# Indexer scores of the last two token tiles over two sets of PSUM banks, and the first convolution slab behind them

## The chip, the cores and the metric

The kernel runs on one core of a Trainium2 chip. The metric is the device time of one launch, in microseconds (us), lower is better; it is given as the median of three runs. The engines are named as the profile names them: PE is TensorE (PEld its weight loads), ACT is ScalarE, DVE is VectorE, POOL is GpSimd, SP the engine that issues the weight loads from memory.

## What is computed

Two layers of a hybrid encoder over 1,072 tokens (1,024 of a prompt, 16 meta tokens, 32 new frames of a running stream). Each layer starts like this:

```python
z = rms_norm(x) @ w_in          # -> q, k, v, indexer qi (4 heads), ki, wi, conv B, C, x, gates A, B
s = einsum('bqhd,bld->bqhl', qi, ki) * IDX_DIM ** -0.5
score = einsum('bqh,bqhl->bql', wi, relu(s))        # sum over the 4 indexer heads
idx = top_k(where(admissible, score, -inf), topk)   # 256 keys (40 for the running stream)
o = attention over the chosen keys                  # branch A
y_b = (cb * causal_conv3(cc * cx)) @ w_conv_out     # branch B
```

The branches are gated, merged and projected, and an MLP (1,024 to 4,096 and back) follows.

## The kernel before

**Layout.** Every engine has its program written out by hand, with semaphores between them; each engine works its own instructions off strictly in the order of the code. Matmuls take fp32r operands, each weight and activation is split into a high and a low part, and three products are added (high by high, high by low, low by high).

**Projection and scores.** The loop `for n in range(9)` in the PE program goes over nine token tiles in the order of `ORDER`: n = 0 is the special tile (meta tokens and stream), then the eight prompt tiles. In turn n, PE runs the projection of tile n + 2 (`proj`, L621, PSUM banks 0 to 2) in four quarters, and between them `turn` (L635: transposes into banks 3 and 4) and `scores` (L651) for the four indexer heads h of tile n. The scores of one head fill up to 1,040 columns from column 2560, that is banks 5 to 7. At n = 7 and n = 8 no projection is left. ACT reads the scores out of PSUM with a relu (`relu_scores`, L1061) into one of two buffers, R0 or R1; DVE multiplies by the head's weight and adds into SC (`add_scores`, L1612 and L1615). PE counts on the semaphore `idx_relu`: the scores of a head wait until the relu of the head before it is done, since both use banks 5 to 7. ACT's program in turn n also copies the projection out of banks 0 to 2 (`copy_out(n + 1)`, semaphore `sb_copied`), copies the transposes, issues stores, and stages the next tile. The copy out of the last tile is the first thing that ACT does in turn n = 7.

**Slabs.** After the scores PE runs 12 convolution slabs and 16 gate slabs (L519, 72 matmuls of 358 columns each, 8 steps of k with 9 matmuls each). Slabs take turns between banks 0 to 2 and 3 to 5. In the kernel before, the first four k steps of slab 0 stand ahead of the scores of tile 8, head 3, and the last four behind them. Slab i waits for its weights (`slab_in`: POOL splits a slab into high and low, L407 and L409, and may start the one for slab 1 only when all 32 adds of the scores are done, `idx_added`), and for its banks: slab 3 waits for DVE's product of `conv_input(0)`, slab 4 for DVE's `conv_gate(0)` (both L1646, semaphore `conv_drained`).

**The search on DVE.** When the last add is done, DVE starts to search the top-k threshold of every row by 31 bits, one pass (L1764, six counts) a bit. The convolution's elementwise work stands at fixed places in that search: `conv_input(j)` and `conv_gate(j)` behind the passes 3j + 2 and 3j + 3 (passes over SC counted from the first bit), `conv_lo_part` between them. The masks that the search gives are read when attention begins, behind the last gate slab. `mask_row` (L1827) is DVE's first step of attention, `logits` (L763) PE's.

Of the kernel before, what the change touches and what calls it, by code (L numbers as in the profile page):

```python
# [21 lines left out]
ALU, ACT, AX = mybir.AluOpType, mybir.ActivationFunctionType, mybir.AxisListType  # L22
# [9 lines left out]
KT = D_MODEL // P  # L32
# [18 lines left out]
S_CONV, S_GATE = 0, NCONV  # L51
# [9 lines left out]
EXT = [N_META + P * (i + 1) for i in range(SPECIAL)] + [MS + PAST]  # L61
# [17 lines left out]
def pieces(t):  # L79

    if t == SPECIAL:
        return [(0, META0, EXT[t])]
    out, c = [(0, META0, N_META)], N_META
    while c < EXT[t]:
        n = min(512 - c % 512, EXT[t] - c)
        out.append((c, c - N_META, n))
        c += n
    return out


def key_tiles(t):

    if t == SPECIAL:
        return [(0, META0, MS, SPECIAL), (MS, PAST0, PAST, SPECIAL + 1)]
    return [(N_META + P * j, P * j, P, j) for j in range(t + 1)] + [(0, META0, N_META, SPECIAL)]
# [29 lines left out]
def edge_no(l, w, i):  # L125

    if l == 0:
        return i
    return 12 * l - 3 + (2 * i + (w == 0) if l < DEPTH else i)


def side(i):
# [10 lines left out]
def build(nc, d):  # L143
    ctx = ExitStack()
    with ctx:
        names = set()

        def sem(name):
            assert name not in names
            names.add(name)  # L150
            return ctx.enter_context(nc.semaphore(name))
# [142 lines left out]
        def ch(ap):  # L294
# [3 lines left out]
        flat = PS[:, :, :].rearrange("p b n -> p (b n)")  # L298
# [9 lines left out]
        slab_done = sem("slab_done")  # L308
# [9 lines left out]
        proj_done, sb_copied, roped, st_hi, st_lo = (  # L318
            sem("proj_done"), sem("sb_copied"), sem("roped"), sem("st_hi"), sem("st_lo"))
# [5 lines left out]
        idx_done, idx_relu, idx_added = sem("idx_done"), sem("idx_relu"), sem("idx_added")  # L325
# [181 lines left out]
        def _(pe):  # L507
            def slab(l, i, s, b0, act, ks=range(KT), signal=True):

                ks = list(ks)  # L510
                for k in ks:
                    last = slab_step(s, b0, act, k, k == ks[0], k == ks[-1])
                last.then_inc(slab_done if signal else half_done, 1)

            def slab_step(s, b0, act, k, first, last):

                for w, a in ((0, 0), (0, 1), (1, 0)):
                    for c in range(NCH):
                        mm = nc.tensor.matmul(PS[:, b0 + c, 0:CW], W[:, s, w, k, :],  # L519
                                              act[:, a, k, c * CW:(c + 1) * CW],  # L520
                                              start=(first and w == 0 and a == 0), stop=(last and w == 1))
                return mm

            def item(w, bank_, j, c, act, ks, first, last):

                for k in ks:
                    for h, a in ((0, 0), (0, 1), (1, 0)):
                        mm = nc.tensor.matmul(PS[:, bank_, 0:CW], w[:, h, k, :], act[:, a, k, c * CW:(c + 1) * CW],  # L528
                                              start=(k == first and h == 0 and a == 0), stop=(k == last and h == 1))
                return mm  # L530
# [35 lines left out]
            def slab_in(l, i):  # L566
                pe.wait_ge(raw_split, l * NRAW + KT + i + 3)
# [33 lines left out]
            for l in range(DEPTH):  # L601
# [26 lines left out]
                def turn(n, blocks, b0, evacs):  # L628

                    m = ROWS[ORDER[n]]  # L630
                    if evacs:
                        pe.wait_ge(turned_out, l * 36 + evacs)
                    for i, blk in enumerate(blocks):
                        o = (b0 + i // 4) * 512 + (i % 4) * P
                        last = nc.tensor.matmul(flat[:, o:o + m], ST[0:m, blk, :], identr[0:m, 0:m],  # L635
                                                start=True, stop=True)
                    last.then_inc(turned, 1)

                def scores(n, h):
                    t = ORDER[n]  # L640
                    m = ROWS[t]
                    if t not in RANKED:
                        return
                    j = RANKED.index(t)
                    if h == 0:
                        pe.wait_ge(turned_out, l * 36 + 4 * n + 2)
                    if 4 * j + h:
                        pe.wait_ge(idx_relu, l * 32 + 4 * j + h)
                    for dst, key, w in pieces(t):
                        for x in range(2):  # L650
                            last = nc.tensor.matmul(flat[0:m, 2560 + dst:2560 + dst + w],  # L651
                                                    IQ[:, h, 0:m], IK[:, x, key:key + w],
                                                    start=(x == 0), stop=(x == 1))
                    last.then_inc(idx_done, 1)
# [23 lines left out]
                for n in range(9):  # L678

                    pe.wait_ge(st_hi, (l * 9 + n + 1) * 3)  # L680
                    pe.wait_ge(st_lo, (l * 9 + n + 1) * 3)
                    turn(n, [8, 9, 10, 11, 12, 13], 3, 4 * n)
                    proj(n + 2, range(0, 2))
                    turn(n, range(8), 3, 4 * n + 2)
                    scores(n, 0)
                    proj(n + 2, range(2, 4))
                    turn(n, range(14, 18), 3, 4 * n + 3)
                    scores(n, 1)
                    proj(n + 2, range(4, 6))
                    scores(n, 2)  # L690
                    proj(n + 2, range(6, 8))
                    if n == 8:
                        slab_in(l, S_CONV)
                        pe.wait_ge(sb_copied, (l + 1) * 9)
                        for k in range(4):
                            slab_step(0, 0, H, k, k == 0, False)
                    scores(n, 3)


                for j in range(4):  # L700
                    for w in range(3):
                        i = 3 * j + w
                        if i == 0:
                            for k in range(4, KT):
                                last = slab_step(0, 0, H, k, False, k == KT - 1)
                            last.then_inc(slab_done, 1)
                            continue
                        slab_in(l, S_CONV + i)

                        if i == 1:  # L710
                            pe.wait_ge(turned_out, (l + 1) * 36)
                            pe.wait_ge(idx_relu, (l + 1) * 32)
                        else:
                            jj, ww = divmod(i - 2, 3)
                            if ww == 0:
                                pe.wait_ge(cc_drained, l * 4 + jj + 1)
                            else:
                                pe.wait_ge(conv_drained, l * 8 + 2 * jj + ww)
                        slab(l, i, i % 2, 3 * (i % 2), H)
# [7 lines left out]
                for s in range(2):  # L727
                    slab_in(l, S_GATE + NGATE - 2 + s)
                    pe.wait_ge(gates_drained, (l + 1) * NGATE - 1 + s)
                    for k in range(KT):  # L730
                        last = slab_step(s, 3 * s, H, k, k == 0, k == KT - 1)
# [70 lines left out]
                for u, (a, kv, kt) in enumerate(STEPS):  # L802
                    i, n = NKV * a + kv, len(key_tiles(ORDER[a]))
# [23 lines left out]
                for k in range(KT):  # L827
                    pe.wait_ge(m_hi, l * NMERGE + k + 1)
                    pe.wait_ge(m_lo, l * NMERGE + k + 1)
                    for c in range(NCH):  # L830
                        last = item(W[:, 0], c, 0, c, H, [k], 0, KT - 1)
                        if k == KT - 1:
                            last.then_inc(item_done, 1)
                for n, (j, c) in enumerate(ITEMS):
# [5 lines left out]
                    last = item(WR[:, j - 1], n % 6, j, c, H, range(KT), 0, KT - 1)  # L840
# [68 lines left out]
                for s in range(2):  # L909
                    slab_in(l, S_MLP + 2 + s)  # L910
                    pe.wait_ge(up_drained, l * NFB * 8 + 2 + s + 1)
                    for k in range(KT):
                        if s == 0 and k == 4:
                            chunk_broadcast(l, 5)
                        last = slab_step(s, 3 * s, H, k, k == 0, k == KT - 1)
# [12 lines left out]
                for k in range(KT):  # L928
                    pe.wait_ge(a_hi, (l * NFB + NFB - 1) * 8 + k + 1)
                    pe.wait_ge(a_lo, (l * NFB + NFB - 1) * 8 + k + 3)  # L930
                    for i in range(NCH):
                        last = item(W[:, 0], i, 0, SIDES[i], A, [k], 0, KT - 1)
# [32 lines left out]
        def _(act):  # L965
# [82 lines left out]
            for l in range(DEPTH):  # L1048
# [3 lines left out]
                def relu_scores(n, h):  # L1052
                    m, t = ROWS[ORDER[n]], ORDER[n]
                    if t not in RANKED:
                        return
                    j = RANKED.index(t)
                    act.wait_ge(idx_done, l * 32 + 4 * j + h + 1)
                    if 4 * j + h >= 2:
                        act.wait_ge(idx_added, l * 32 + 4 * j + h - 1)
                    dst = (R0, R1)[h % 2]  # L1060
                    nc.scalar.activation(dst[0:m, 0:EXT[t]], flat[0:m, 2560:2560 + EXT[t]], ACT.Relu)\  # L1061
                        .then_inc(idx_relu, 1)

                def copy_out(n):
# [55 lines left out]
                for n, t in enumerate(ORDER):  # L1120
                    m, nn = ROWS[t], l * 9 + n
# [28 lines left out]
                    for h in range(1, NIDX):  # L1150
                        relu_scores(n, h)
# [66 lines left out]
                for u, (a, kv, kt) in enumerate(STEPS):  # L1218
                    t, now = ORDER[a], NKV * a + kv
                    m, w, n = ROWS[t], key_tiles(t)[kt][2], len(key_tiles(t))  # L1220
# [39 lines left out]
                for s in range(2):  # L1260
                    n = l * NMERGE + NMERGE - 2 + s
# [835 lines left out]
```

## Time and profile before

| what | value |
|---|---|
| median of three runs | 3534.87 us (3533.64 to 3535.16) |
| profiled execution, own time | 3524.78 us |
| profiled execution, span | 3523.0 us |
| mean granted TensorE clock | 0.968 of full |
| PE busy | 3345.7 us, 95% of the span |
| DVE, POOL, ACT busy | 1876.1, 1123.8, 769.5 us |
| scores (L651) | 336 matmuls, two layers |
| relu of scores (L1061) | 64 activations, median 0.655 us |

A line of the timeline gives the start and the length of a group of instructions, the engine, the source line, the operation and its shapes, and in brackets how long the engine had stood idle before it and who ended the idle time. The granted clock is told as a share: 1.00 is 2.4 GHz, 0.50 is 1.2 GHz. The scores of the last two tiles of the first layer lie at about 217 to 250 us of the span, those of the second layer at about 1953 to 1988 us.

### The profile page before, as it was taken

Reading aid. Unit: us, or ns where it says so; the run is one execution under the profiler, and the core shown is the slowest. Engines: PE = TensorE matmul, PEld = TensorE weight load, DVE = VectorE, ACT = ScalarE, POOL = GpSimd, SP = SyncE. Lnnn points to the kernel's source line nnn. Section 1 sums busy time; section 2 is a strip of 40 time slices with the busy share of each in tenths; the row PEclk is TensorE's granted clock in tenths of the full one; section 3 lists DMA queues with packets and bytes.
Section 4 is the critical chain, followed back from the end, with each engine's and each line's share of the span. In section 5 each row is a group of like instructions: output and inputs, shape, how many; then the busy total and the mean of one; then the engine's idle time right before and its main releaser. Section 6 shows DMA issues by size and latency. Waiting matters only on the chain.

```text
span 3523.0 us, 49297 instructions
## 1 busy us (share of the span) xinstructions
PE 3345.7 (95%) x19604; PEld 3177.9 (90%) x19604; DVE 1876.1 (53%) x3093; ACT 769.5 (22%) x1368; POOL 1123.8 (32%) x517
## 2 busy tenths in 40 slices
PE   4989998999999999999969899989999999999997
PEld 3989998669999999999969899976699999999997
DVE  5249997654563242415562599966446623333255
ACT  4330111560330010101233201125413201001011
POOL 2013333004544343434420233320045434344360
PEclk8989998999999999999989899979999999999998
DMA  3111223003321111111331112220133211111113
GB/s 124 49 55 42 67 86 122 25 7 136 110 75 42 45 45 42 48 42 48 103 98 56 53 42 80 85 103 25 41 110 99 79 48 42 48 42 48 42 60 101
DMA packets 95743, 230.00 MB, mean 65 GB/s; under 512 B 11921, under 2 KB 52465, under 8 KB 95601
## 3 DMA queue, kind: packets, MB, share of 16 engines
q1 hardware_dynamic: 33552, 122.57, 11.1%
q10 hardware_dynamic: 62048, 105.48, 8.6%
q8 instruction: 97, 1.59, 0.2%
q14 instruction: 46, 0.37, 0.0%
HBM read 176.37 MB, written 51.65 MB: 65 GB/s over the span
## 4 chain that ended last, share of the span: by engine, by line
PE 86%; DVE 7%; ACT 2%; issue 2%; DMA 2%; POOL 1%; ACTq 1%; DVEq 0%; POOLq 0%
PE PS L519 58%; PE PS L528 9%; PE PS L621 6%; PE PS L792 5%; PE PS L763 3%; PE PS L780 2%; PE PS L651 2%; DVE PASS L1764 1%; PE PS L635 1%; DVE X L1538 1%; DVE HN L1493 1%; DMA HN<-x_keep 1%; DVE X L1544 1%; ACT SB L967 1%; DVE H L1489 1%
## 5 line engine op out<-in xcount | busy, mean ns | idle before, releaser
L519 PE MATMUL PS<-H,W 128*128 128x358 f32 x8352 | 1385.9, 328 | 11.3 <-DVE CB L1646 7.3
L519 PEld LDWEIGHTS PS<-H,W 128*128 128x128 f32 x8352 | 1381.3, 190 | 13.2 <-issue 10.3
L407 POOL TENSOR_TENSOR W<-RAW,ones 128x1024 fp32r<-128x1024 f32 x188 | 365.7, 1945 | 2051.7 <-PE PS L519 1664.6
L519 PE MATMUL PS<-A,W 128*128 128x358 f32 x4608 | 760.9, 327 | 0.0
L519 PEld LDWEIGHTS PS<-A,W 128*128 128x128 f32 x4608 | 759.5, 189 | 1.5 <-issue 1.5
L409 POOL TENSOR_TENSOR W<-RAW,W 128x1024 fp32r<-128x1024 f32 x188 | 522.0, 2777 | 14.8
L1764 DVE TENSOR_SCALAR_CACHE_REDUCE PASS<-SC,TC,CST 128x400 bf16<-128x400 f32 x372 | 356.0, 1019 | 1.7
L621 PE MATMUL PS<-WQ,H 128*128 128x364 f32 (+1 forms) x1296 | 244.3, 345 | 45.7 <-ACT SB L967 38.5
L621 PEld LDWEIGHTS PS<-WQ,H 128*128 128x128 f32 (+1 forms) x1296 | 218.4, 190 | 57.8 <-ACT SB L967 41.4
L1927 DVE TENSOR_TENSOR SQ<-SQ,RS 128x1074 f32<-128x1074 f32 x64 | 117.8, 1840 | 266.0 <-ACT SQ L1338 260.2
L1338 ACT ACTIVATE SQ<-PS 128x1074 f32<-128x1074 f32 x64 | 68.4, 1068 | 811.2 <-PE PS L519 808.9
L1929 DVE TENSOR_TENSOR SQ<-SQ 128x1074 f32<-128x1074 f32 x64 | 205.1, 3204 | 2.2
L1942 DVE TENSOR_TENSOR X<-X,PS 128x1074 f32 x32 | 40.8, 1274 | 307.3 <-PE PS L519 307.3
L792 PE MATMUL PS<-PT,V 128*128 128x512 f32 (+3 forms) x368 | 197.9, 621 | 0.3
L763 PEld LDWEIGHTS PS<-KS,QS 128*128 128x128 f32 (+1 forms) x704 | 116.9, 208 | 82.5 <-issue 65.8
L763 PE MATMUL PS<-KS,QS 128*128 128x16 f32 (+6 forms) x704 | 169.8, 371 | 13.0 <-issue 8.0
L528 PE MATMUL PS<-A,WD 128*128 128x358 f32 x1008 | 168.1, 327 | 0.0
L528 PE MATMUL PS<-H,WR 128*128 128x358 f32 x1008 | 168.0, 326 | 0.0
L528 PEld LDWEIGHTS PS<-A,WD 128*128 128x128 f32 x1008 | 165.1, 188 | 0.0
L528 PEld LDWEIGHTS PS<-H,WR 128*128 128x128 f32 x1008 | 164.5, 188 | 0.0
L967 ACT ACTIVATE PT<-PS 128x512 f32<-128x512 f32 (+3 forms) x184 | 107.4, 583 | 187.9 <-PE PS L780 187.8
L967 ACT ACTIVATE A<-SQ 128x1074 f32 (+1 forms) x64 | 70.6, 1103 | 340.9 <-DVE SQ L1929 340.9
(176 smaller groups left out, 2859.3 us busy)
## 6 DMA issues: line engine op xcount, KB each, us to landing
RAW<-in_w_slab SPq DMA_DIRECT2D x216, 512.0 KB, 3.5
gates<-GS ACTq DMA_DIRECT2D x32, 537.0 KB, 3.0
x_keep<-X ACTq DMA_DIRECT2D x9, 1432.0 KB, 7.6
RAW<-in_w_qkv SPq DMA_DIRECT2D x16, 546.0 KB, 3.6
GA<-gates ACTq DMA_DIRECT2D x16, 537.0 KB, 3.7
GB<-gates ACTq DMA_DIRECT2D x16, 537.0 KB, 4.6
ALO<-x_keep ACTq DMA_DIRECT2D x6, 1432.0 KB, 7.5
qs_keep<-QH ACTq DMA_DIRECT2D x16, 512.0 KB, 2.6
```

The source lines that it names most:

```text
L407: g_.tensor_tensor(hi, raw, one, ALU.mult).then_inc(hi_split, 1)
L409: g_.tensor_tensor(lo, raw, hi.bitcast(F32), ALU.subtract).then_inc(raw_split, 1)
L519: mm = nc.tensor.matmul(PS[:, b0 + c, 0:CW], W[:, s, w, k, :], act[:, a, k, c * CW:(c + 1) * CW], start=(first and w == 0 and a == 0), sto ...
L528: mm = nc.tensor.matmul(PS[:, bank_, 0:CW], w[:, h, k, :], act[:, a, k, c * CW:(c + 1) * CW], start=(k == first and h == 0 and a == 0), st ...
L621: last = nc.tensor.matmul(PS[0:m, b, 0:QG], H[:, a, k, t * P:t * P + m], WQ[:, k, w, b * QG:(b + 1) * QG], start=(k == 0 and w == 0 and a ...
L651: last = nc.tensor.matmul(flat[0:m, 2560 + dst:2560 + dst + w], IQ[:, h, 0:m], IK[:, x, key:key + w], start=(x == 0), stop=(x == 1))
L763: last = nc.tensor.matmul(flat[0:m, c0 + dst:c0 + dst + w], QS[:, a % 3, GROUP * kv + q, 0:m], KS[:, 2 * kv + x, key:key + w], start=(x == ...
L792: nc.tensor.matmul(PS[:, 6 + kv, 0:GROUP * m], V[0:w, vt, :], PT[0:w, u % 3, 0:GROUP * m], start=(kt == 0), stop=(kt == len(key_tiles(t)) ...
L967: return nc.scalar.activation(out, in_, ACT.Copy)
L1764: did(V_.tensor_scalar(PASS[0:m, SC_OFF[t]:SC_OFF[t] + EXT[t]], row(t), at_least, cst["negk"][0:m, c:c + 1], op, ALU.add, accum_out=CNT[0: ...
L1927: V_.tensor_tensor(SQ[:, s, :], SQ[:, s, :], RS[:, :], ALU.mult).then_inc(up_scaled, 1)
L1929: V_.tensor_tensor(SQ[:, s, :], SQ[:, s, :], SQ[:, s, :], ALU.mult).then_inc(up_sq, 1)
```

## The change

Of the tiles n = 7 and n = 8, heads 1 and 3 write their scores to banks 0 to 2 (column 0 on), heads 0 and 2 stay in banks 5 to 7. ACT's relu reads from the same column. The wait of these scores is loosened by one: from the second head of tile 7 on, a head waits for the relu before the last one. The first head that writes to banks 0 to 2 waits for the last copy out of the projection. Slab 0 is no longer cut in two: it stands whole behind the last scores and waits for all 32 relus of the layer.

```diff
+def score_col(n, h):
+
+    return 0 if n >= 7 and h % 2 else 2560
...
                     if h == 0:
                         pe.wait_ge(turned_out, l * 36 + 4 * n + 2)
+                    if n == 7 and h == 1:
+                        pe.wait_ge(sb_copied, (l + 1) * 9)
                     if 4 * j + h:
-                        pe.wait_ge(idx_relu, l * 32 + 4 * j + h)
+                        pe.wait_ge(idx_relu, l * 32 + 4 * j + h - (4 * n + h > 28))
                     for dst, key, w in pieces(t):
                         for x in range(2):
-                            last = nc.tensor.matmul(flat[0:m, 2560 + dst:2560 + dst + w],
+                            last = nc.tensor.matmul(flat[0:m, score_col(n, h) + dst:score_col(n, h) + dst + w],
...
                     proj(n + 2, range(6, 8))
-                    if n == 8:
-                        slab_in(l, S_CONV)
-                        pe.wait_ge(sb_copied, (l + 1) * 9)
-                        for k in range(4):
-                            slab_step(0, 0, H, k, k == 0, False)
                     scores(n, 3)
...
                         if i == 0:
-                            for k in range(4, KT):
-                                last = slab_step(0, 0, H, k, False, k == KT - 1)
-                            last.then_inc(slab_done, 1)
+                            slab_in(l, S_CONV)
+                            pe.wait_ge(idx_relu, (l + 1) * 32)
+                            slab(l, 0, 0, 0, H)
                             continue
...
-                    nc.scalar.activation(dst[0:m, 0:EXT[t]], flat[0:m, 2560:2560 + EXT[t]], ACT.Relu)\
+                    nc.scalar.activation(dst[0:m, 0:EXT[t]], flat[0:m, score_col(n, h):score_col(n, h) + EXT[t]], ACT.Relu)\
```

## Rows read from the trace of the kernel before

**Rows 1.** The page: its head, and the chain that ended last, by engine.
```profile
span 3523.0 us, 49297 instructions
...
PE 86%; DVE 7%; ACT 2%; issue 2%; DMA 2%; POOL 1%; ACTq 1%; DVEq 0%; POOLq 0%
```
**Rows 2.** The chain that ended last, 205 to 305 us: start, length, what.
```profile
243.19 6.91 PE PS L519 x36
...
252.47 1.31 DVE SC L1615
...
297.42 1.47 DVE CB L1646 x4
```
**Rows 3.** Waits of PE, 215 to 310 us: total, times, longest.
```profile
PE PS L651 <- ACT R L1061: 4.2, 5, 1.6
PE PS L519 <- DVE CB L1646: 3.6, 1, 3.6
...
PE PS L519 <- POOL W L409: 1.0, 1, 1.0
PE PS L519 <- DVE CU L1646: 0.9, 1, 0.9
```
**Rows 4.** Timeline of PE, tiles 7 and 8, first layer.
```profile
219.47 2.29 PE L651 MATMUL PS<-IK,IQ 128*128 128x16 f32 x6 [0.28 <-ACT R L1061]
...
223.39 2.29 PE L651 MATMUL PS<-IK,IQ 128*128 128x16 f32 x6 [1.64 <-ACT R L1061]
...
240.49 2.70 PE L651 MATMUL PS<-IK,IQ 128*128 128x16 f32 x8 [1.13 <-ACT R L1061]
243.04 7.05 PE L519 MATMUL PS<-H,W 128*128 128x358 f32 x36
249.93 1.42 PE L651 MATMUL PS<-IK,IQ 128*128 128x16 f32 x8
251.21 6.17 PE L519 MATMUL PS<-H,W 128*128 128x358 f32 x36
```
**Rows 5.** Timeline of ACT and POOL, tiles 7 and 8, first layer.
```profile
213.95 1.07 ACT L967 ACTIVATE SB<-PS 128x1092 f32<-128x1092 f32 x1
...
222.43 0.91 ACT L1061 ACTIVATE R<-PS 128x912 f32<-128x912 f32 x1
...
238.54 2.68 POOL L409 TENSOR_TENSOR W<-RAW,W 128x1024 fp32r<-128x1024 f32 x1
```
**Rows 6.** Stretches of 1 us: busy time of PE, PEld, DVE, ACT, POOL, then granted clock.
```profile
233.00:234.00 1.00, 1.00 (x5) 0.92 (x5) 0.00 (x0) 0.87 (x1) 0.00 (x0) 0.50 0.00 0
...
245.00:246.00 1.00, 1.00 (x8) 1.00 (x8) 0.60 (x1) 0.00 (x0) 0.00 (x0) 0.99 0.00 0
```
**Rows 7.** Timeline of PE, slabs 1 and 2, slab 3, slab 4 and on.
```profile
258.40 23.98 PE L519 MATMUL PS<-H,W 128*128 128x358 f32 x144 [1.02 <-POOL W L409]
283.31 12.10 PE L519 MATMUL PS<-H,W 128*128 128x358 f32 x72 [0.93 <-DVE CU L1646]
299.02 121.25 PE L519 MATMUL PS<-H,W 128*128 128x358 f32 x725 [3.61 <-DVE CB L1646]
```
**Rows 8.** Timeline of POOL and DVE at the ends of slabs 3 and 4.
```profile
295.56 1.91 POOL L407 TENSOR_TENSOR W<-RAW,ones 128x1024 fp32r<-128x1024 f32 x1 [8.36 <-PE PS L519]
295.76 1.74 DVE L1787 SCALAR_TENSOR_TENSOR TC<-TU,TC 128x8 uint32<-128x8 uint32 x1
...
304.78 0.17 DVE L1787 SCALAR_TENSOR_TENSOR TC<-TU,TC 128x8 uint32<-128x8 uint32 x1
...
312.73 1.90 POOL L407 TENSOR_TENSOR W<-RAW,ones 128x1024 fp32r<-128x1024 f32 x1 [12.81 <-PE PS L519]
```
**Rows 9.** Timeline of PE, second layer, first half of slab 0.
```profile
1979.69 7.40 PE L519 MATMUL PS<-H,W 128*128 128x358 f32 x36
```
**Rows 10.** Waits of PE, second layer, 1950 to 2052 us.
```profile
PE PS L519 <- DVE CB L1646: 3.7, 1, 3.7
```
**Rows 11.** Timeline of DVE, its first step of attention.
```profile
587.55 0.33 DVE L1827 CUSTOM_DVE_ANT_0 PA<-PS,MB 48x176 f32<-48x176 f32 x1 [5.12 <-PE PS L763]
```

## Prediction

> **What bounds the kernel now.** I read the page first: PE is on 86% of the chain that ended last, DVE on 7% [rows 1]. So time comes out of this kernel where PE idles or runs slowly, and the question is who makes it do so between the last projection and the slabs. The chain between 205 and 305 us says it: it goes through the first half of slab 0 (243.19, 6.91 us), then through the scores of tile 8, head 3, their relu and their add (252.47, 1.31 us), and then stays on DVE's search until `conv_gate(0)` (297.42, 1.47 us) [rows 2]. The reader is to see that the half slab that fills PE's wait for a relu also holds back the last add, from which DVE's whole search starts, and that slab 4 then waits for that search. The waits of PE give the sizes: 4.2 us in five waits of scores for relus, 1.0 us of slab 1 for its weights, 0.9 and 3.6 us of slabs 3 and 4 for DVE [rows 3]. The clock is the second finding: through tiles 7 and 8 PE runs at 1.2 GHz, also in a stretch in which it is busy throughout (233 to 234 us), and full clock is back at 245 us, some 2 us into slab 0 [rows 6].
>
> **What it removes, one layer.** (a) The five waits of scores for the relu of the head before: 4.2 us [rows 3]. Can the looser wait be met? Head 1 of tile 7 starts 0.28 us earlier, at 219.2 [rows 4]; its banks are free, since the last copy out began at 213.95 and took 1.07 us [rows 5]. Head 2 follows at about 221.5, by 2.29 us a head, head 3 at 223.8. Head 3 needs the relu of head 1, which ACT starts at 222.43 (it stages a tile before it, so this relu comes no earlier) and ends at 223.34 [rows 5]: just in time. In tile 8 a head takes 2.7 us on PE and the relu about 1.05 us on ACT [rows 2 and 4], so the relu before the last is always done. I take the whole 4.2.
> (b) Slab 1's wait, 1.0 us [rows 3]. Its weights can be split only after the last add. That add ends at 253.78 now [rows 2]; with scores of head 3 ahead of the slab it ends about 10 us earlier (below), and the split ends before slab 0 does.
> (c) DVE's chain. From the last add's end at 253.78 to the end of `conv_gate(0)` at 298.89 it takes 45.1 us [rows 2]. In the kernel after, slab 0 starts as the last relu ends, and the last add ends 1.3 us after that, so `conv_gate(0)` ends 46.4 us after slab 0 starts. Slab 4 is due after four slabs: slabs 1 and 2 take 23.98, slab 3 takes 12.10 [rows 7], so 48 us at full clock and about 2 us more for the start at half clock: 50. DVE is 3.6 us early, and both waits go: 0.9 + 3.6 = 4.5 us [rows 3].
> (d) What follows the wait of slab 4. Slab 3 runs from 283.31 to POOL's release at 295.56, 12.25 us; slab 4 from 299.02 to 312.73, 13.7 us [rows 7 and 8]. The only difference is that slab 4 starts after 3.61 us of idle PE. With that idle gone 1.4 us come back.
> Removed: 4.2 + 1.0 + 4.5 + 1.4 = 11.1 us.
>
> **What it adds, one layer.** (e) The scores of tile 8, head 3 now run in the half clock stretch. At half clock eight of these matmuls hold PE from 240.49 to 243.04, 2.55 us; now they hold it at full clock from 249.93 to 251.21, 1.28 us [rows 4]. Added 1.3 us.
> (f) A new wait: slab 0 waits for the relu of the scores just ahead of it. The same wait for the same size of relu stands in the row before slab 0 and lasts 1.13 us [rows 4]. Behind it on PE are all the slabs, so nothing fills it: 1.1 us. The weights of slab 0 are no wait: POOL ends their split at 241.22 now [rows 5], some 3 us earlier when the transposes before them are, against a slab start at about 242.4.
> (g) The clock at the start of the slab. Now the first half of slab 0 takes 7.05 us against 6.17 for the second half, a loss of 0.9; in the second layer 7.40, a loss of 1.2 [rows 4 and 9]. After an idle wait the loss may be like slab 4's 1.4 (d). Below, I take 0.9 again as the least; above, twice slab 4's, 2.8, since the wait comes at the end of a half clock stretch and not after full clock. I take 2.0, between, so 1.1 more than now in the first layer and 0.8 in the second.
> Added: 1.3 + 1.1 + 1.0 = 3.4 us.
> (h) Slab 0 uncut costs nothing: it has the same 72 matmuls. The wait for `sb_copied` costs nothing (a). The DMAs are as before; the weights for slab 1 can only come earlier. ACT's order is the same.
>
> **Sum.** 11.1 − 3.4 = 7.7 us a layer. As a check by places: slab 0 starts at 243.04 − 4.2 + 2.55 + 1.1 = 242.5; slab 4 at 292.5 instead of 299.02, and it ends 1.4 us sooner relative to its start, 7.9 us in all. The second layer shows the same waits, with 3.7 us for slab 4 [rows 10], and loses less at (g): 8.1 us. Together 16 us. Behind slab 4 PE runs 121 us and more without a wait [rows 7], so the gain is carried on. The masks must be ready at the start of attention: there DVE has waited 5.12 us for PE's first logits [rows 11]. DVE moves up by at least as much as PE, since it starts 10 us earlier and meets PE again at each later `conv_input`. The sum is made in the profiled execution, 3524.78 us with a span of 3523.0; the median of the runs is 3534.87, 10.1 us above it. I take the difference over unscaled: 3534.87 − 16 = 3519.
>
> **A page against the rows.** The rows show PE busy throughout and still at half clock [rows 6]; it was transposing and scoring. The Trainium skill, page "TensorE: Matmul & The Clock Gate", section "What's actually happening", says that the throttled state is the default and that activity releases it; by that rule alone closing the waits of (a) could bring full clock back among the scores, and the sum would be that of rival A. The row speaks against it for a busy PE of this mix, but no stretch of this trace has three heads in a row without a wait.
>
> **Rivals.**
> A. *Full clock comes back while PE still scores.* In the kernel after, heads 1 to 3 of tile 7 run without a gap, which no row shows. For: it is denser than anything here before slab 0. Against: the busy stretch at 0.50. Price: a head of tile 8 holds PE 1.28 instead of 2.55 us [rows 4]; with four of them, ACT's copies in between become the wait, and I count some 3 of the 5 us; the 2.0 of (g) goes as well. 5 us more a layer, 3509 with both layers, 3514 with one. It is not more, because DVE's 46.4 us then stand against 48 for PE.
> B. *DVE's chain gets longer and binds.* While POOL splits (295.56, 1.91 us) a small DVE operation took 1.74 instead of 0.17 us [rows 8]. Where such meetings fall changes with the change. Three more of them cost 3 × 1.6 = 4.8 us, 1.2 over the margin of 3.6, with 1.4 again for an idle start of slab 4; the gain is 5 to 7 us a layer, 3521 to 3525. On this, the Trainium skill, page "SBUF — State Buffer", section "SBUF: two separate sides", tells of a port pair that DVE and GpSimd lock against each other for a whole instruction; the trace agrees with 1.74 us beside 1.91.
> C. *Slower: half clock stays deep in the slabs.* The new wait (f) puts idle time right ahead of the dense work. Every us at half clock costs half a us, so the change is a loss once more than some 16 us a layer beyond the 4 us of (g) run at 1.2 GHz; slower by 7 us at 23. It would give 3542. Against: both starts of slab 0 and that of slab 4 lost at most 1.4 us.
> D. *The waits only move.* Head 3 of tile 7 meets the relu by less than half a us (a). If ACT's staging holds each relu back, 2 of the 4.2 us stay, and the gain is 6 us a layer: 3523.
>
> **How the numbers follow.** Forecast, the sum with (g) between its bounds (3516 to 3522): 0.65. A: 0.16. B and D: 0.13. C: 0.02. Nothing measurable, for a reason that I don't see, 0.04. 0.2%, about what a measurement of this kernel can tell from no change, is 7.1 us, under half of the sum; B and D still lie beyond it. So faster 0.93, same 0.05, slower 0.02. The range from 3510 to 3526 takes in (g)'s bounds, B and D and most of A.
>
> **What would show it.** The waits of L651 for R gone at tiles 7 and 8; one wait of about 1.1 us before slab 0 at about 242.5; the last add ended at about 243.8 (c); no wait of L519 for POOL, CU or CB; slab 4 at about 292.5 and of 12 us; granted clock 0.50 until 2 to 5 us into slab 0. Waits of L519 for CB would show B, full clock before slab 0 A, waits for R at tile 7 D. The forecast is wrong if DVE's chain from the last add is over 48 us, or if PE's idle time turns up again later, ahead of attention.

## The result, and the profile after

The kernel after took 3509.6 us (median of 4 runs, 3503.4 to 3510.4) beside 3534.8 us before (4 runs, 3533.6 to 3535.2): ratio 0.9926, interval 0.9908 to 0.9943. The direction was right, the size was not: 16 us were forecast, 25 came, and 3509.6 lies just outside the range, below its end of 3510. Run twice more on other occasions the kernel gave ratios of 0.9922 (0.9905 to 0.9939) and 0.9939 (0.9925 to 0.9953). Over all 16 executions its mean is 3508.8 us, over 63 of the kernel before 3533.0: 24.2 us.

The line numbers move: the scores are L658 now, the slabs L524, POOL's splits L412 and L414, the relu L1063, DVE's CU and CB L1648. The page of the kernel after, its head and the chain by engine, which answer to [rows 1]:

```profile
span 3508.1 us, 49299 instructions
...
PE 88%; DVE 5%; ACT 2%; issue 2%; DMA 1%; POOL 1%; ACTq 1%; DVEq 0%; POOLq 0%
```

DVE has lost 2 points of the chain, PE has gained them. The waits of PE in the first layer, 212 to 320 us:

```profile
PE PS L640 <- ACT IK L969: 3.8, 2, 2.0
PE PS L524 <- ACT R L1063: 2.6, 1, 2.6
PE PS L658 <- ACT R L1063: 0.8, 2, 0.4
```

and those of the second layer, 1938 to 2060 us:

```profile
PE PS L640 <- ACT IK L969: 3.0, 2, 2.0
PE PS L524 <- ACT R L1063: 1.2, 1, 1.2
PE PS L658 <- ACT R L1063: 0.3, 1, 0.3
```

Beside [rows 3] and [rows 10]: the waits for POOL, CU and CB are gone in both layers, the relu waits of the scores have shrunk from 4.2 us to 0.8 us in the first layer and 0.3 in the second, and the one new wait, slab 0 for the last relu, is 1.2 us in the second layer, as forecast, but 2.6 in the first. The timeline of PE says why. First layer, the kernel after:

```profile
219.92 3.96 PE L658 MATMUL PS<-IK,IQ 128*128 128x16 f32 x12
224.33 1.31 PE L658 MATMUL PS<-IK,IQ 128*128 128x16 f32 x6 [0.45 <-ACT R L1063]
...
230.74 2.83 PE L658 MATMUL PS<-IK,IQ 128*128 128x16 f32 x16
233.88 1.52 PE L658 MATMUL PS<-IK,IQ 128*128 128x16 f32 x8 [0.31 <-ACT R L1063]
238.04 92.25 PE L524 MATMUL PS<-H,W 128*128 128x358 f32 x542 [2.64 <-ACT R L1063]
```

Head 3 of tile 7 (224.33) takes 1.31 us where it took 2.29: from here on PE is at full clock while it still scores, which is rival A. Slab 0 starts at 238.04, 5 us before [rows 4] and 4.5 us before the forecast 242.5. The relu that it waits for was itself held, by DVE's adds. The timeline of POOL, DVE and ACT:

```profile
232.96 2.71 POOL L414 TENSOR_TENSOR W<-RAW,W 128x1024 fp32r<-128x1024 f32 x1
233.86 5.71 DVE L1617 SCALAR_TENSOR_TENSOR SC<-R,WI,SC 128x1040 f32<-128x1040 f32 x3 [0.43 <-ACT R L1063]
236.86 1.04 ACT L1063 ACTIVATE R<-PS 128x1040 f32<-128x1040 f32 x1 [2.10 <-DVE SC L1617]
```

At full clock PE outruns the adds, and R0 and R1 come free too late: ACT waits 2.10 us, PE 2.64. The first of the three adds of L1617 takes 2.90 us, the next 1.30. POOL's split of slab 0's weights (232.96 to 235.67) runs beside the slow one, so 1.6 of the 2.10 us that ACT waits are the length that this add has over the next. It is the kind of meeting that rival B names, in a place where B did not look for it. The wait costs more than its length. Stretches of 1 us of the same execution, columns as in [rows 6]:

```profile
237.00:238.00 1.00, 0.00 (x0) 0.00 (x0) 1.00 (x1) 0.90 (x1) 0.00 (x0) 0.59 0.56 176
243.00:244.00 1.00, 1.00 (x5) 1.00 (x4) 0.93 (x4) 0.00 (x0) 1.00 (x1) 0.50 0.00 0
244.00:245.00 1.00, 1.00 (x8) 1.00 (x7) 0.90 (x4) 0.00 (x0) 0.16 (x1) 0.99 0.00 0
```

While PE idles the clock falls, and slab 0 runs its first 6 us at half clock.

**How the runs are compared below.** Every run lists its span and its mean granted clock. Span × clock is the time that the execution would have taken if every stretch at half clock had been half as long; span × (1 − clock), half the time at half clock, is called below what it lost to half clock. This is bookkeeping and not yet a cause: idle time at half clock falls half into each part, though a higher clock would not shorten it. The listed clock has three digits, so one run's split is good to about 2 us, a mean's to less.

| kernel | runs | mean us | span × clock | lost to half clock (runs) |
|---|---|---|---|---|
| before | 63 | 3533.0 | 3408.0 | 123.2 (116 to 134) |
| after | 16 | 3508.8 | 3393.7 | 113.3 (101 to 123) |
| order only | 7 | 3520.0 | 3398.0 | 120.1 (112 to 127) |
| banks only | 12 | 3525.6 | 3403.7 | 120.1 (105 to 138) |
| tile 8 only | 6 | 3520.9 | 3396.5 | 122.6 (120 to 127) |
| tile 7 only | 6 | 3516.4 | 3396.9 | 117.7 (112 to 123) |
| swapped banks | 4 | 3499.3 | 3392.6 | 104.9 (98 to 112) |
| before + filler | 12 | 3529.0 | 3413.2 | 114.1 (106 to 120) |
| after + filler | 4 | 3497.0 | 3406.0 | 89.1 (87 to 95) |
| swapped + filler | 4 | 3497.3 | 3401.1 | 94.4 (87 to 98) |

So of the 24.2 us, 14.3 are in the first part and 9.9 in the second. The 9.9 are not all a gain of clock. The relu waits stood at half clock, so about half of the 8.4 us of them is in it. So are the 3 us that slab 4 ran at half clock behind its wait (granted clock 0.81, 0.50, 0.50 and 0.50 from 299 to 303 us before, 1.00 throughout slab 4 in the third profile below), 1.6 us lost in each layer. What the half clock among the scores gave or took beside these is smaller than the scatter of single executions.

### The profile page after: what moved, and what is told of

The parts are those of the page before. It is cut to its first block, busy times and chain, and to the rows that moved or that the text cites. A ratio compares the mean times of both kernels' runs of the same rounds, so it can differ in the third digit from the quotient of the medians.

```text
span 3508.1 us, 49299 instructions
## 1 busy us (share of the span) xinstructions
PE 3348.5 (95%) x19604; PEld 3181.8 (91%) x19604; DVE 1873.5 (53%) x3093; ACT 769.0 (22%) x1368; POOL 1123.9 (32%) x517
## 4 chain that ended last, share of the span: by engine, by line
PE 88%; DVE 5%; ACT 2%; issue 2%; DMA 1%; POOL 1%; ACTq 1%; DVEq 0%; POOLq 0%
PE PS L524 61%; PE PS L533 9%; PE PS L626 6%; PE PS L794 5%; PE PS L765 3%; PE PS L782 2%; PE PS L658 1%; PE PS L640 1%; DVE X L1540 1%; DVE HN L1495 1%; DVE X L1546 1%; DMA HN<-x_keep 1%; ACT SB L969 1%; DVE H L1491 1%; DVE H L1535 0%
## 5 line engine op out<-in xcount | busy, mean ns | idle before, releaser
L524 PE MATMUL PS<-H,W 128*128 128x358 f32 x8352 | 1383.3, 328 | 3.9 <-ACT R L1063 3.9
L524 PEld LDWEIGHTS PS<-H,W 128*128 128x128 f32 x8352 | 1380.8, 189 | 4.1 <-issue 4.0
L412 POOL TENSOR_TENSOR W<-RAW,ones 128x1024 fp32r<-128x1024 f32 x188 | 365.9, 1946 | 2037.7 <-PE PS L524 1674.9
L524 PE MATMUL PS<-A,W 128*128 128x358 f32 x4608 | 760.9, 327 | 0.0
L524 PEld LDWEIGHTS PS<-A,W 128*128 128x128 f32 x4608 | 759.5, 189 | 1.5 <-issue 1.5
L414 POOL TENSOR_TENSOR W<-RAW,W 128x1024 fp32r<-128x1024 f32 x188 | 521.7, 2775 | 14.7
L1929 DVE TENSOR_TENSOR SQ<-SQ,RS 128x1074 f32<-128x1074 f32 x64 | 117.7, 1839 | 266.2 <-ACT SQ L1340 260.2
```

Source lines behind the costliest of these rows:

```text
L412: g_.tensor_tensor(hi, raw, one, ALU.mult).then_inc(hi_split, 1)
L414: g_.tensor_tensor(lo, raw, hi.bitcast(F32), ALU.subtract).then_inc(raw_split, 1)
L1929: V_.tensor_tensor(SQ[:, s, :], SQ[:, s, :], RS[:, :], ALU.mult).then_inc(up_scaled, 1)
```

## The experiments

**The two kernels again.** No edit. The profiled execution from which the forecast was made took 3524.8 us, 10 less than its timed runs, so I wanted to know whether that was chance.

> The kernel before, unchanged, profiled again. Its timed runs lay at 3533.6 to 3535.2 us, its profiled execution at 3524.8, so 10 us of the 25 us that the change gained are not in the trace from which the sum was made. Theory P (the profiled execution was a lucky one): a second profile comes out near 3534 us and shows those 10 us in some stretch, most likely as half clock among the scores or at the start of attention. Theory Q (profiling itself makes this kernel faster): the second profile is again near 3525 us.

Measured: ratio 0.9996 (0.9987 to 1.0005) to the kernel before, runs from 3526.1 to 3539.1 us; its profiled execution took 3528.1. Neither theory as put: the second profile is neither near 3534 nor near 3525. The median, 3532.2, lies near the earlier timed runs, so the first profile was a fast draw, as P says. The span and clock of the first profile, 3523.0 and 0.968, give 113 us lost to half clock, less than any of the 63 later executions (116 to 134); its span × clock, 3410.3, is an ordinary one. Against the second profile, which lost 120 us, the difference lies in attention. Stretches of 250 us that hold it, one for each layer, for the first profile of before (columns as in [rows 6], with the stretch's length behind its bounds):

```profile
570.00:820.00 250.00, 233.96 (x1162) 168.09 (x1161) 137.84 (x376) 115.81 (x258) 19.08 (x8) 0.94 0.15 52
2290.00:2540.00 250.00, 235.78 (x1139) 167.77 (x1138) 144.56 (x385) 115.76 (x258) 18.09 (x7) 0.92 0.15 51
```

and for the second profile:

```profile
570.00:820.00 250.00, 235.94 (x1140) 167.72 (x1139) 135.55 (x375) 115.88 (x258) 16.45 (x6) 0.92 0.15 52
2290.00:2540.00 250.00, 236.89 (x1138) 168.45 (x1138) 148.28 (x387) 118.18 (x260) 20.82 (x8) 0.91 0.13 45
```

The clock in attention differs between two executions of the same program, 0.94 and 0.92 in the first layer, 0.92 and 0.91 in the second; together that is some 7 us. One profile is one draw of it.

> The kernel after, unchanged, profiled again. Theory 1 (the gain is 16 us of waits and clock as summed, plus what the profile of before did not show): median 3509 to 3510 us and a profile within 7 us of it, with full clock among the scores in no, one or both layers. If the run at 3503.4 us comes again, its profile has full clock before slab 0 in both layers.

Measured: 3504.0 us median (3498.0 to 3515.1), 5 us below theory 1's; the profiled one took 3507.5. Its first layer had full clock from 224 to 227.7 us among the scores and again from 237.4 us, so that slab 0 (from 240.87) ran wholly at full clock; its second layer had none before slab 0. What the runs at 3498 to 3501 us had, no profile shows.

> The kernel after once more, for comparison on the same chip: 3504 to 3510, about 3394 us of the span times the granted clock and about 110 us lost to half clock.

Measured: 3512.8 us median (3507.0 to 3516.2) and 117.6 us lost to half clock on average, both above what was expected; 3392.7 in the first part, as expected. This profile is the one in which the forecast can be checked as it was made, since the clock did not come back among the scores in either layer. Timeline of PE, first layer:

```profile
219.14 4.15 PE L658 MATMUL PS<-IK,IQ 128*128 128x16 f32 x12
223.55 2.29 PE L658 MATMUL PS<-IK,IQ 128*128 128x16 f32 x6 [0.26 <-ACT R L1063]
...
233.13 7.71 PE L658 MATMUL PS<-IK,IQ 128*128 128x16 f32 x24
242.06 88.19 PE L524 MATMUL PS<-H,W 128*128 128x358 f32 x525 [1.22 <-ACT R L1063]
```

Timeline of POOL, which starts a split when a slab before it is done; and the product of `conv_gate(0)` in that of DVE:

```profile
243.38 1.99 POOL L412 TENSOR_TENSOR W<-RAW,ones 128x1024 fp32r<-128x1024 f32 x1 [5.29 <-DVE SC L1617]
...
279.41 1.89 POOL L412 TENSOR_TENSOR W<-RAW,ones 128x1024 fp32r<-128x1024 f32 x1 [7.43 <-PE PS L524]
...
291.34 1.91 POOL L412 TENSOR_TENSOR W<-RAW,ones 128x1024 fp32r<-128x1024 f32 x1 [7.55 <-PE PS L524]
...
303.14 1.90 POOL L412 TENSOR_TENSOR W<-RAW,ones 128x1024 fp32r<-128x1024 f32 x1 [7.43 <-PE PS L524]
```

```profile
283.94 1.46 DVE L1648 TENSOR_TENSOR CB<-PS,CY 128x716 f32<-128x716 f32 x4
```

Slab 0 at 242.06 (forecast 242.5), last add done at about 243.3 (243.8), slab 4 from 291.34 (292.5) to 303.14, 11.80 us. DVE's product is done at 285.40, 42 us after the last add, 5.9 us before slab 4 needs it (3.6 were forecast). From 228.0 to 240.8 us PE is listed busy without a gap and the granted clock is 0.50 all the way; full clock comes back at 245.1, 3 us into slab 0.

**Order only.** Slab 0 uncut behind the scores, all scores in banks 5 to 7. It needs no relu, since it writes to banks 0 to 2.

```diff
-                    if n == 8:
-                        slab_in(l, S_CONV)
-                        pe.wait_ge(sb_copied, (l + 1) * 9)
-                        for k in range(4):
-                            slab_step(0, 0, H, k, k == 0, False)
...
-                            for k in range(4, KT):
-                                last = slab_step(0, 0, H, k, False, k == KT - 1)
-                            last.then_inc(slab_done, 1)
+                            slab_in(l, S_CONV)
+                            pe.wait_ge(sb_copied, (l + 1) * 9)
+                            slab(l, 0, 0, 0, H)
```

> Only the second part of the change: slab 0 uncut behind the scores of tile 8, head 3; all scores stay in banks 5 to 7 and wait for each relu. Slab 0 needs no relu, since its banks 0 to 2 are free. By the terms of the sum: last add some 4.5 us earlier than before, slab 4 at about 296.5 instead of 299.0 us of the profile, 4 us a layer, 8 us in all, 3526. Rival (a lone DVE chain): slab 4 moves by all that the last add moves, 4.5 us, with the clock's 1.4 us, 12 us in all, 3523.

Measured: ratio 0.9964 (0.9952 to 0.9977), 3518.1 us median, 13.0 us by means. More than the 8 of the sum, and 1 more than the rival's 12, so it is the rival's account that fits: slab 4 moves by all that the last add moves. All waits of PE from 212 to 320 us:

```profile
PE PS L651 <- ACT R L1056: 5.4, 6, 1.6
PE PS L635 <- ACT IK L962: 3.0, 2, 2.0
```

There is one relu wait more than in [rows 3], and no wait of a slab at all. The half slab ahead of the last scores was what made slabs 1, 3 and 4 wait; putting it behind them is enough to end that. The clock did not help here: in the first layer it stayed at 0.50 from 217.8 to 251.6 us, 3 us into slab 0 (from 248.62), longer than before.

**Banks only.** The scores of tile 8, head 3 stay in banks 5 to 7 behind the half slab, and the half slab waits for the relu of head 1.

```diff
+    return 0 if n >= 7 and h % 2 and (n, h) != (8, 3) else 2560
...
-                        pe.wait_ge(idx_relu, l * 32 + 4 * j + h)
+                        pe.wait_ge(idx_relu, l * 32 + 4 * j + h - (28 < 4 * n + h < 35))
...
-                        pe.wait_ge(sb_copied, (l + 1) * 9)
+                        pe.wait_ge(idx_relu, l * 32 + 30)
                         for k in range(4):
```

> Only the first part: heads 1 and 3 of tile 7 and head 1 of tile 8 in banks 0 to 2, the scores of tile 8, head 3 stay in banks 5 to 7 behind the half of slab 0, which waits for the relu of head 1. By the terms of the sum: the 4.2 us of waits go, the last add and slab 4 come 4 us earlier, and the 3.6 us wait of slab 4 stays, 8.4 us in all, 3526. If full clock comes back among the scores as in the first layer of the kernel after (rival A of the prediction), 3 to 5 us a layer more, 3517 to 3520.

Measured: ratio 0.9981 (0.9967 to 0.9995), 3524.8 us median, 7.4 us by means, near the 8.4 of the sum. Its waits in the first layer:

```profile
PE PS L524 <- DVE CB L1653: 3.6, 1, 3.6
PE PS L640 <- ACT IK L974: 3.0, 2, 2.0
PE PS L524 <- POOL W L414: 1.0, 1, 1.0
PE PS L524 <- DVE CU L1653: 0.9, 1, 0.9
PE PS L658 <- ACT R L1068: 0.3, 1, 0.3
```

The relu waits go and the three slab waits stay to the tenth of a us: the whole stage moves up, nothing in it shrinks. In span × clock the parts add up within their error of about 1 us: 10.0 (order) and 4.3 (banks) beside 14.3 (both), and 4.3 is what 8.4 us of waits at half clock should leave there, 4.2. In the clock they give 3.1 each and both 9.9, but single executions scatter there by 15 to 30 us, and with 7 and 12 runs I don't hold that difference for settled.

**One tile alone.** The kernel after with the turns between banks kept to tile 8 (first edit) or to tile 7 (second).

```diff
+    return 0 if n == 8 and h % 2 else 2560        # tile 8 only; wait loosened for 4 * n + h > 32
...
+    return 0 if n == 7 and h % 2 else 2560        # tile 7 only; wait loosened for 28 < 4 * n + h < 33
```

> The kernel after, but only tile 8 takes turns between the banks; the scores of tile 7 stay in banks 5 to 7 and wait for every relu. 2.9 us of waits a layer stay. Theory A (it is tile 7's three heads without a gap that bring full clock back among the scores in some layers): the clock's gain is gone, the part of the span lost to half clock is 118 to 124 us as before instead of about 110, and the time is 3514 to 3522. Rival B (the clock gains from tile 8 or from the uncut slab): lost part near 112, time 3508 to 3512.

> The counterpart: only tile 7 takes turns, tile 8 stays in banks 5 to 7 and waits for every relu, 2.4 us a layer. Theory A: the lost part stays near 110 and a stretch of full clock stands among the scores of the first layer, as in the kernel after; time 3508 to 3512. Rival B: lost part 118 to 124, time 3514 to 3522.

Measured: tile 8 only 0.9966 (0.9954 to 0.9978), tile 7 only 0.9950 (0.9937 to 0.9964). The comparison has to stay within the session, in which the kernel before lost 123.3 us (11 runs) and the kernel after 117.6 (6 runs). Tile 8 only lost 122.6, as theory A says. Tile 7 only lost 117.7, as much as the kernel after, which also speaks for A; but its time, 3518.1 us median, lies in B's range, and its profile, of one of the two executions that lost most (123.1), has no full clock among the scores. So leaving tile 7 as it was takes the gain in the second part away, by 5 us with an error of about 2; that this gain comes from full clock among tile 7's scores is not shown. Both kernels show the price of waits: PE waits 2.9 and 2.7 us a layer for relus instead of 0.3; at half clock half of that is in span × clock, 2.6 and 2.4 us for two layers, and 2.8 and 3.2 over the kernel after were measured (3.8 and 4.2 over its 6 runs of the same session).

**Filling the waits.** To move the clock by itself I added matmuls whose results nobody reads into PE's idle time, here in the kernel before:

```diff
+                def filler(bank_, n):
+                    for _ in range(n):
+                        nc.tensor.matmul(PS[:, bank_, 0:CW], H[:, 0, 0, 0:P], H[:, 0, 0, 0:CW],
+                                         start=True, stop=True)
...
                     proj(n + 2, range(0, 2))
+                    if n == 7:
+                        pe.wait_ge(idx_relu, l * 32 + 24)
+                        filler(5, 9)
+                    if n == 8:
+                        pe.wait_ge(sb_copied, (l + 1) * 9)
+                        filler(0, 5)
                     turn(n, range(8), 3, 4 * n + 2)
```

> The kernel before, with matmuls added that compute nothing used, in PE's idle time: 9 of 358 columns into bank 5 in the 2.03 us wait ahead of the second transposes of tile 7, 5 into bank 0 in the 0.96 us wait at tile 8. Scores, slabs and waits are as before. Theory K (the clock is the mis-sized term: PE loses about 13 us a layer to 1.2 GHz from this wait on until slab 0): granted clock stays or comes back to 1.00 among the scores, the share of the span lost to half clock falls by 10 to 20 us in all, the rest of the span stays at 3408, and the time goes to 3513 to 3525. Rival W (waits alone matter): 14 more matmuls a layer change nothing or cost 2 to 3 us, 3533 to 3537.

Measured: ratio 0.9990 (0.9981 to 0.9999), 3529.1 us median, 4 us by means, between the two theories. The clock followed: 9.1 us less lost. But 5.2 of them came back in the other part, against the expectation that it stays at 3408. Waits of PE for relus, first layer:

```profile
PE PS L651 <- ACT R L1073: 6.3, 5, 2.6
```

They were 4.2 us. With the scores faster, PE reaches the same relu earlier and waits longer. The fillers themselves held the transposes up by at most 0.4 us a layer. The clock alone pays little while the relu chain binds.

> The kernel after with such added matmuls, 9 in the wait of tile 7, 8 in that of tile 8, 8 into bank 3 in the wait before slab 0. Theory K: full clock from tile 7 into slab 0 in both layers, slab 0 some 4 us earlier in the layer that had half clock, no half clock in slab 0: 3490 to 3500. Rival W: 3504 to 3510 as the kernel after, or 1 to 3 us more where the fillers outlast the waits.

Measured: 3496.6 us median (3491.2 to 3503.5), ratio 0.9898 (0.9883 to 0.9912). Stretches of the second layer, this kernel and then the kernel after:

```profile
1930.00:2060.00 130.00, 125.25 (x760) 122.07 (x759) 104.61 (x221) 23.52 (x32) 41.70 (x20) 1.00 0.17 54
```

```profile
1930.00:2060.00 130.00, 125.50 (x690) 121.90 (x689) 102.65 (x213) 24.60 (x34) 38.66 (x18) 0.88 0.16 53
```

(The second is from the second profile of that kernel.) Granted clock 1.00 in place of 0.88. In the first layer theory K did not hold in this execution, the slowest of the four: its clock was at 0.50 from 224.0 to 230.6 us, among the scores. By means 24 us less are lost over the whole run, and 12 of them given back. Some 5 of the 12 are a wait of 2.5 us in each layer, of head 3 of tile 7 for a relu behind ACT's staging; where the others went I did not trace. The waits of PE, the same in both layers:

```profile
PE PS L658 <- ACT R L1077: 2.8, 2, 2.5
PE PS L524 <- ACT R L1077: 1.2, 1, 1.2
```

**Swapped banks.** Even heads in banks 0 to 2, odd ones in banks 5 to 7, so that slab 0 needs the relu of head 2 only.

```diff
-    return 0 if n >= 7 and h % 2 else 2560
+    return 0 if n >= 7 and h % 2 == 0 else 2560
...
-                            pe.wait_ge(idx_relu, (l + 1) * 32)
+                            pe.wait_ge(idx_relu, l * 32 + 31)
```

The first wait for `sb_copied` moves to head 0 of tile 7, and the loosened wait starts there.

> The kernel after with the banks the other way round: heads 0 and 2 of tiles 7 and 8 in banks 0 to 2, heads 1 and 3 in banks 5 to 7. Slab 0 then needs only the relu of tile 8, head 2, and starts right behind the last scores. Theory 1 (the 1.2 to 2.6 us wait before slab 0 is a pure loss): slab 0 begins 1 to 2.6 us earlier in each layer, 2 to 5 us in all, 3500 to 3504 beside 3504 to 3510 for the kernel after. Rival (DVE's chain of 45 us from the last add takes over): slab 4 gets a wait for CB of the same size, and the time stays at 3504 to 3508.

Measured: 3499.5 us median (3496.5 to 3502.0), ratio 0.9913 (0.9898 to 0.9927), a little under the lower end of theory 1 and outside the rival's range. Timeline of PE, second layer:

```profile
1956.20 7.71 PE L658 MATMUL PS<-IK,IQ 128*128 128x16 f32 x24
1963.76 11.55 PE L524 MATMUL PS<-H,W 128*128 128x358 f32 x65
```

The new wait is gone, and no slab waits for CB. In span × clock this is worth 1.1 us (3392.6 beside 3393.7), about the half of two waits of 1.2 us that ought to stand there; the other 8.4 us by which its mean lies under that of the kernel after are in the part that scatters, and the two kernels were not run in the same session. So it is faster than the kernel before; that it beats the kernel after by more than a few us is not shown.

> The kernel of the swapped banks with 9 added matmuls in the wait of tile 7 and 8 in that of tile 8, none before slab 0, where nothing is to fill. Theory K: full clock throughout, slab 0 starts right behind the last scores, and DVE's chain then binds slab 4 by 1 to 2 us: 3488 to 3498, at most 3 us under the kernel after with fillers. Rival W: as the swapped banks alone, 3500 to 3508.

Measured: 3499.8 us median (3488.7 to 3500.9), ratio 0.9913 (0.9899 to 0.9927), the profiled execution 3488.7. The median lies just between the ranges of the two theories, and only the profiled run is in K's. DVE's chain, which K expected to hold slab 4 by 1 to 2 us, did not: no slab waits for CB in either layer. No gain over either edit alone that these runs can tell.

## Why the prediction was wrong

**Right in mechanism.** What bounded the stage, (a) to (d), was read rightly. The waits of the scores for R went but for 0.3 us, and all three slab waits went. "Order only" shows that the half slab held DVE's search and through it slab 4, "banks only" that the relu waits are a separate 4.2 us. The new wait (f) is 1.2 us where the clock stayed as forecast. Slab 0 and slab 4 came within 0.5 and 1.2 us of their places. DVE's chain took 42 us instead of 45.1, so B did not come. That was luck in part: DVE operations that run beside a POOL split take longer than the same ones without it (the 1.74 us beside 0.17 of [rows 8]; one of 3.36 us at 284.97 that took 1.34 in the third profile). Such excesses add up to some 6 us in the chain before and to some 3 us in the chain after, since the meetings fell otherwise. The masks were ready as before. C did not come.

**Wrong in size.** The step that failed is the size of three terms, each of which made the gain too small: the waits (a) with the idle starts behind (b) to (d), the clock at slab 0 (g), and the clock among the scores, which the sum kept at 1.2 GHz. (The sum also adds (g) with 1.0 where its own text has 1.1, which changes nothing here.)

*The clock among the scores, rival A.* The sum let PE run at 1.2 GHz through tiles 7 and 8 and counted the clock only at the start of slab 0. In two of three profiles of the kernel after, the first layer got full clock back among the scores. From the start of the last projection matmul to the first logits that layer took 375.1 us before (211.9 to 587.0), 362.6 in the first profile after (212.1 to 574.7), and 365.4 in the third, with half clock throughout (212.1 to 577.5): 12.5 and 9.7 us less. So A's place was right, and its price was 3 us and not 5. In the first profile slab 0 started 4.0 us earlier than in the third, but where A let the 2.0 of (g) go as well, the clock fell again in the wait for the held relu: from slab 0's start to POOL's next split 14.88 us passed, beside 13.62 in the third profile and 12.19 in the second, in which slab 0 ran at full clock. Its chance should have been larger: I gave 0.16 on one busy 1 us row at 0.50, in which PE was transposing as well as scoring, while the change makes three heads run gaplessly. By the Trainium skill's rule of activity, page "TensorE: Matmul & The Clock Gate", section "What's actually happening", the prediction had the right rival in hand; the second layer of the same executions, at half clock over the same instructions, and the 12.8 us of the third profile in which PE was listed busy at 0.50, show that the rule does not say by itself when.

*The waits, (a), the idle starts behind (b) to (d), and (g).* Even where the clock stayed as forecast, the first layer gained 9.7 us instead of 7.7, and the second 10.3 instead of 8.1 (377.0 us before, 366.7 in the third profile, between the same two points). In the first layer the 2 us can be placed. Idle time in a timeline is counted from the modelled end of a matmul. Starts tell more. In the kernel before, tile 8's head 2 started at 240.49 [rows 4], 3.83 us behind head 1:

```profile
236.66 2.70 PE L651 MATMUL PS<-IK,IQ 128*128 128x16 f32 x8 [0.18 <-ACT R L1061]
```

In the third profile of the kernel after, without the wait, the relus of these heads follow each other by 2.53 us (timeline of ACT):

```profile
235.81 1.04 ACT L1063 ACTIVATE R<-PS 128x1040 f32<-128x1040 f32 x1 [1.84 <-PE PS L658]
238.34 1.04 ACT L1063 ACTIVATE R<-PS 128x1040 f32<-128x1040 f32 x1 [1.50 <-PE PS L658]
```

That is 1.3 us for a wait listed as 1.13, and slab 0 came 0.5 us earlier than forecast. A slab that starts after an idle wait takes 12.25 us from its start to POOL's next split ([rows 7 and 8], slab 3), and one that follows another without idle time 11.80 or 11.93 by turns. The sum counted the idle time of slabs 1, 3 and 4 and the half clock of slab 4, and left out these 0.3 to 0.4 us of each start, 1 us in all. And (g) was put at 2.0 us where it was 1.4 (13.62 us for slab 0 in the third profile, against 12.25; 13.77 in the second layer).

**The baseline.** The difference was taken from an execution that had lost 113 us to half clock, beside 123 on average. It did not bias the sum much, since the lucky stretches lie in attention, outside it. But it hid how far executions of one kernel differ, 116 to 134 us lost, and that the measured medians carry it.

**The account.** By means 24.2 us were gained, 8.2 over the forecast. About 4.2 are the mis-sized waits, idle starts and (g) (2.0 and 2.2 us in the layers without full clock), about 2 the full clock in the first layer (3 us in two of three profiles). The other 2 us are not placed, and the cause of these stays open. They may be chance in attention's clock, which in 250 us stretches stood at 0.88 to 0.91 in the first layer of the kernel after and at 0.92 and 0.94 before, that is, no gain there that a profile shows. Why full clock comes back in one layer and not in the other I did not find out.

## What to carry to other kernels

Work put ahead of a short wait to fill it also delays everything behind that wait: ask which engine's long chain starts there before asking what the filler saves. Measure what a removed wait is worth from start to start of the instructions around it and not from the listed idle time. And split every run into span × clock and span × (1 − clock): the first part answered to within 1 us and added up over the parts of the change, while the second scattered by 15 us and more from one execution to the next and needs many runs. The split does not say what a better clock would bring: with fillers the second part fell by 9 and 24 us, and 5 and 12 us came back in the first.

## What was not expected of the hardware

The same instructions at the same point of the same program ran at full clock in one execution and at half clock in the next: head 3 of tile 7 took 1.31 us at 224.33 in one profile of the kernel after and 2.29 us at 223.55 in another. In both PE was listed busy without a gap from 216.0 to about 223.3 or later, behind the same idle wait of 2.03 us; in the first the clock had fallen at about 216.9 and rose at about 223.5, in the other it fell at about 217.9 and stayed down. And a higher clock gave back only a part of what it seemed to promise: in "after + filler" 24 us less were lost to half clock and 12 more were spent on the rest, since the work between the matmuls did not get faster with PE's clock: the relu of 1,040 columns took 1.04 us at 0.50 and at 1.00 alike.
